# Chunked delta-rule scan: product order, PSUM banks, activation tables and a moved residual add

## The reference

```python
def step(S, xs):
    qk_i, qd_i, kd_i, u_i, w_i, gl_i = xs
    v_new = u_i - jnp.einsum('bhid,bhde->bhie', w_i, S)
    o_i = jnp.einsum('bhid,bhde->bhie', qd_i, S) + jnp.einsum('bhij,bhje->bhie', qk_i, v_new)
    S = S * gl_i[..., None, None] + jnp.einsum('bhid,bhie->bhde', kd_i, v_new)
    return S, o_i

S0 = jnp.zeros((B, H, dk, dv), q.dtype)
...
o_dn = o_dn * lax.rsqrt(jnp.mean(jnp.square(o_dn), axis=-1, keepdims=True) + RMS_EPS)
...
return jnp.concatenate([o_attn, o_dn], axis=-1) @ w_out
...
h = layer_norm(DEEPNORM_ALPHA * h + mix, ln1_g, ln1_b)
ffn = peer_ffn(h, peer_w_query, peer_sub_keys, peer_u, peer_v)
h = layer_norm(DEEPNORM_ALPHA * h + ffn, ln2_g, ln2_b)
```

## Time and profile before

| | |
|---|---|
| median of 3 runs | 3115.99 us (3113.97 to 3116.4) |
| the profiled execution | 3117.14 us |
| its span, first to last instruction | 3115.3 us |
| PE, DVE, ACT, POOL busy | 2386.0, 2232.4, 1148.3, 1183.5 us |
| gathers (queue q0) | 1073.81 MB, 83.5% of the DMA engines' span |
| other loads (q1) | 154.32 MB, 12.6% |
| mean granted TensorE clock | 0.877 of full speed |

### The profile page before, as it was taken

One profiled execution on the slowest core, in us unless ns is written; L12 is line 12 of the kernel. 1 busy time (PEld: TensorE's weight loads), 2 busy tenths in 40 slices (PEclk: granted clock), 3 DMA queues, 4 the chain that ended last, 5 costly groups with the idle time before them and its releaser, 6 DMA issues.

```text
span 3115.3 us, 37879 instructions
## 1 busy us (share of the span) xinstructions
PE 2386.0 (77%) x11858; PEld 1345.3 (43%) x11858; DVE 2232.4 (72%) x5639; ACT 1148.3 (37%) x3506; POOL 1183.5 (38%) x1028
## 2 busy tenths in 40 slices
PE   8897778868789687877879778886878668785554
PEld 7684435434356343543446443542435324351111
DVE  5388656986579766797568966689656986678644
ACT  4123533354323533235333353324533354333222
POOL 0033442344423444234533445234542344434442
PEclk9999989889899797888888889888989879888777
DMA  8189999999999999999999999999999999999997
GB/s 348 41 345 418 420 419 403 402 417 420 420 404 406 420 415 416 408 386 420 420 407 414 413 420 422 401 389 407 420 420 404 402 416 420 416 386 419 411 422 311
DMA packets 189000, 1235.90 MB, mean 397 GB/s; under 512 B 21752, under 2 KB 21880, under 8 KB 54656
## 3 DMA queue, kind: packets, MB, share of 16 engines
q0 software_dynamic: 147456, 1073.81, 83.5%
q1 hardware_dynamic: 39168, 154.32, 12.6%
q10 hardware_dynamic: 2176, 5.36, 0.4%
HBM read 1229.21 MB, written 4.19 MB: 396 GB/s over the span
## 4 chain that ended last, share of the span: by engine, by line
PE 31%; DVE 31%; DMA 20%; ACT 7%; issue 7%; POOL 2%; another core or an unknown queue 1%; DVEq 0%; ACTq 0%; POOLq 0%; SPq 0%
DMA ring<-in_uv,expert_used 18%; DVE ring L1823 14%; PE expert_sum L989 13%; PE bank L612 7%; PE bank L601 2%; POOL ring L539 2%; ACT diag L1314 2%; PE bank L619 2%; DVE arena L1454 1%; DMA chunk<-in_weights 1%; PE bank L593 1%; DVE conv L1474 1%; PE bank L742 1%; DVE arena L1469 1%
## 5 line engine op out<-in xcount | busy, mean ns | idle before, releaser
L539 POOL DMA_INDIRECT ring<-in_uv,expert_used x1024 | 1183.3, 1156 | 1895.4 <-PE expert_sum L989 1387.0
L989 PE MATMUL expert_sum<-ring,diag 128*64 128x512 f32 x4096 | 1185.3, 708 | 623.9 <-ACT diag L1314 618.9
L1823 DVE CUSTOM_DVE_ANT_0 ring<-ring,x_pair 128x1024 f32<-128x1024 f32 x1024 | 1221.4, 1223 | 357.2 <-DMA ring<-in_uv,expert_used 351.5
L989 PEld LDWEIGHTS expert_sum<-ring,diag 128*64 128x64 f32 x4096 | 308.7, 154 | 1246.2 <-issue 1230.3
L1307 ACT ACTIVATE h_raw<-h_raw 128x2 f32<-128x2 f32 x512 | 104.2, 204 | 1341.8 <-DVE h_raw L1823 1320.0
L1314 ACT ACTIVATE diag<-const,h_raw 128x64 f32<-128x64 f32 x1024 | 292.8, 333 | 6.2 <-PE expert_sum L989 5.8
L1310 ACT ACTIVATE h_raw<-h_raw,gate_used 128x1 f32<-128x1 f32 x1024 | 245.6, 286 | 16.7
L612 PEld LDWEIGHTS bank<-oT,chunk 128*128 128x128 f32 x1344 | 152.7, 192 | 22.7 <-issue 22.7
L612 PE MATMUL bank<-oT,chunk 128*128 128x128 f32 x1344 | 158.6, 277 | 0.0
L1454 DVE MAX8 arena<-arena 128x8 f32<-128x128 f32 (+1 forms) x384 | 103.8, 326 | 48.4 <-ACT arena L1260 43.1
L601 PE MATMUL bank<-chunk,oT 128*128 128x256 f32 x464 | 109.7, 387 | 0.0
(11 more groups left out here) (275 smaller groups left out, 2715.1 us busy)
## 6 DMA issues: line engine op xcount, KB each, us to landing
chunk<-in_weights SPq DMA_DIRECT2D x228, 512.0 KB
ring<-in_weights SPq DMA_DIRECT2D x17, 1024.0 KB, 23.8
ring<-in_uv,expert_used POOLq DMA_INDIRECT x1024
chunk<-in_weights SPq DMA_DIRECT2D x4, 1024.0 KB, 20.7
x<-in_x SPq DMA_DIRECT2D x8, 512.0 KB
out<-oT ACTq DMA_DIRECT2D x8, 512.0 KB
o_cat<-in_xT SPq DMA_DIRECT2D x7, 512.0 KB
xT_even<-in_xT SPq DMA_DIRECT2D x4, 512.0 KB
```

Source lines behind the costliest of these rows:

```text
L539: pool.indirect_dma_start(out=place(n, j), out_offset=None, in_=io["uv"], in_offset=bass.IndirectOffsetOnAxis(ap=expert_used[:, j:j + 1], ...
L989: mm = pe.matmul(expert_sum[i][c * SPAN:(c + 1) * SPAN, :], diag[:, (j % DIAGS) * SPAN:(j % DIAGS + 1) * SPAN], place(n, j)[:, D + i * 512 ...
L1823: dve.tensor_tensor_reduce(u, u, x_pair[:, (j % 2) * D:(j % 2 + 1) * D], 1.0, 0.0, ALU.mult, ALU.add, h_raw[:, j:j + 1]).then_inc(dotted.s ...
```

## The change

PE issues Q.S right behind W.S, before it waits for the subtraction, and each head's output gets a bank of its own (`O_BANKS`), so that Q.S of all heads comes first and QK.V of all heads later. In chunk 0 K.V comes before QK.V, in chunk 1 behind it. DVE's state update waits for Q.S (`q_state`) in place of QK.V. ACT copies four pieces, one from each bank. In block 0, chunk 0, the state is zero: W.S, Q.S and the subtraction are left out, and A_U is used as v_new. `add_half` of block 0 moves behind `dn_out` in DVE's queue. Ahead of the wait for each of the three roots ACT gets an instruction that loads a table set named `natural_log_exp_and_others`.

```diff
+        O_BANKS = (2, 0, 1, 5)
@@ PE, scan
-                bw, bo, bk = 3, 2, 4
+                bw, bk = 3, 4
                 for c in range(2):
                     rows = slice(c * CHUNK, (c + 1) * CHUNK)
                     if c == 0:
@@
                         pe.wait_ge(*state_new.at(n, 1))
                         pe.wait_ge(*o_copied.at(n, 1))
-                    each_head(bank[bw], tile(A_WT), state[:, :]).then_inc(w_state.sem, 1)
+                    from_zero = early and c == 0
+                    if from_zero:
+                        pe.sem_inc(w_state.sem, 1)
+                        pe.sem_inc(q_state.sem, 1)
+                    else:
+                        each_head(bank[bw], tile(A_WT), state[:, :]).then_inc(w_state.sem, 1)
+                        for h in range(DH):
+                            hs = slice(h * P, (h + 1) * P)
+                            mm = pe.matmul(bank[O_BANKS[h]][:, 0:P], tile(A_QDT)[:, hs], state[:, hs], start=True, stop=False)
+                        mm.then_inc(q_state.sem, 1)
                     mark(("ws0", "ws1")[c])
                     spare(early, (2, 1)[c])
                     pe.wait_ge(*v_new.at(n, c + 1))
+                    vn = tile(A_U) if from_zero else tile(A_VN)
+
+                    def into_state():
+                        for h in range(DH):
+                            hs = slice(h * P, (h + 1) * P)
+                            mm = pe.matmul(bank[bk][:, hs], tile(A_KDEC)[rows, hs], vn[rows, hs], start=True, stop=True)
+                        mm.then_inc(kv_done.sem, 1)
+
+                    if c == 0:
+                        into_state()
                     for h in range(DH):
                         hs = slice(h * P, (h + 1) * P)
-                        mm = pe.matmul(bank[bk][:, hs], tile(A_KDEC)[rows, hs], tile(A_VN)[rows, hs], start=True, stop=True)
-                    mm.then_inc(kv_done.sem, 1)
-                    for h in range(DH):
-                        hs = slice(h * P, (h + 1) * P)
-                        pe.matmul(bank[bo][:, hs], tile(A_QDT)[:, hs], state[:, hs], start=True, stop=False)
-                        mm = pe.matmul(bank[bo][:, hs], tile(A_QKT)[rows, hs], tile(A_VN)[rows, hs], start=False, stop=True)
+                        mm = pe.matmul(bank[O_BANKS[h]][:, 0:P], tile(A_QKT)[rows, hs], vn[rows, hs], start=from_zero, stop=True)
                     mm.then_inc(o_done.sem, 1)
+                    if c == 1:
+                        into_state()
@@ ACT, scan and roots
-                    act.copy(tile(A_O)[rows, :], bank[2][rows, :]).then_inc(o_copied.sem, 1)
+                    for h in range(DH):
+                        ins = act.copy(tile(A_O)[rows, h * P:(h + 1) * P], bank[O_BANKS[h]][rows, 0:P])
+                    ins.then_inc(o_copied.sem, 1)
@@
+                act.preload_act_table_set("natural_log_exp_and_others")
                 act.wait_ge(*o_ms.at(n, 1))
@@
+                act.preload_act_table_set("natural_log_exp_and_others")
                 act.wait_ge(*var_ready.at(n, 1))
@@ DVE, scan
-                    dve.wait_ge(*solved_copied.at(n, 1))
-                    dve.wait_ge(*w_state.at(n, c + 1))
-                    tt(tile(A_VN)[rows, :], tile(A_U)[rows, :], bank[bw][rows, :], ALU.subtract).then_inc(v_new.sem, 1)
+                    if n == 0 and c == 0:
+                        dve.sem_inc(v_new.sem, 1)
+                    else:
+                        dve.wait_ge(*solved_copied.at(n, 1))
+                        dve.wait_ge(*w_state.at(n, c + 1))
+                        tt(tile(A_VN)[rows, :], tile(A_U)[rows, :], bank[bw][rows, :], ALU.subtract).then_inc(v_new.sem, 1)
                     mark(("ws0", "ws1")[c])
                     dve.wait_ge(*kv_done.at(n, c + 1))
-                    dve.wait_ge(*o_done.at(n, c + 1))
+                    dve.wait_ge(*q_state.at(n, c + 1))
@@
-                if n == 0:
-                    add_half(0, expert_sum)
                 dve.wait_ge(*o_copied.at(n, 2))
@@
                 tt(by_head(o_cat[:, 512:1024]), by_head(tile(A_O)), over_cols(col(S_RT, DH), P), ALU.mult).then_inc(dn_out.sem, 1)
+                if n == 0:
+                    add_half(0, expert_sum)
```

More of the change, by code:

```diff
@@ L343, in build @@
         w_state = signal("w_state", 2)
+        q_state = signal("q_state", 2)
         v_new = signal("v_new", 2)
```

## The result

The changed kernel takes **3095.19 us** (median of 4 runs, 3092.87 to 3100.25) against 3116.19 for the kernel before beside it (3113.97 to 3119.75): a ratio of 0.9939, 95% interval 0.9926 to 0.9953, so 21.0 us faster. The forecast was 3106.6 with a range down to 3101: right in direction, and short by half. The profiled execution took 3092.87 us, 24.3 less than that of before.

The account below looks back on a forecast made before the run. Bytes pace 2915 us between a latency chain before 166 us and a latency tail. Gains 7.6 (block 0) + 1.3 (tail) + 0.5 (middle) = 9.4 us, from the median 3115.99 to 3106.6 us; range 3101 to 3112.

Parts of the forecast that it names:

- Block 0: Start of the kernel, up to the first gather: 6.8 us at the transposes and 0.8 at the first norm, 7.6 together.
- the output transposes: Block 0, behind the scan: 6.8 us earlier, taken between 5.9 and 7.1.
- the norm: Block 0's first norm: its table load goes, but keep-busy matmuls stand before x1's transposes, so -0.8 us, not -1.28.
- Tail: End of the kernel: the table load between Ln and Exp of the last norm goes, -1.3 us.
- Scan stages: Scans of blocks 1 to 7: DMA share stays at 1.0, time saved there is spent waiting for the next gather.
- The middle: The 2915 us paced by bytes, between first and last gather: -0.5 us.
- I take -0.5: The value in us chosen for the part paced by bytes, as the saved loads and scan lie beside transfers.
- an earlier norm does not bring that gather earlier: Turns between blocks: DVE last waits 1.9 to 2.6 us for the old block's gather before making the new indices.
- The upper bound: Part paced by bytes, at best: seven turns following the norm, 9.0 us, and a stretch such as 1572 to 1587, 2.6.
- the middle gains too: Rival, chance 0.10: the turns follow the earlier norm, sum 18.4 us or half of the 9.0, 3098 to 3102 us.
- The rule on the most contended engine: Whole kernel: a change that leaves DMA alone gives nothing, 3116 us; said to agree for the middle, not before 166 us.
- the limit of telling: Whole kernel: a measurement can tell 0.2%, 6.2 us, so faster means below 3109.8 us.

Follow-up runs that it names:

- root_after_turn: The kernel before with the table set of both functions loaded ahead of the second norm's root only: 3111.37 us, ratio 0.9993.
- after_norm_late: The changed kernel with the load ahead of the first norm replaced in blocks 1 to 7 by two loads behind the variance wait: 3098.80 us, ratio 0.9955.
- after_sums_late: The changed kernel with VectorE reading the expert sums twice at the turns into blocks 1 to 7: 3112.65 us, ratio 0.9999.
- after_again: The changed kernel itself measured once more, nothing changed: 3096.78 us, ratio 0.9949.

## Why the prediction was right at the ends and wrong in the middle

- **Block 0, right.** 7.6 us were forecast, 8.0 measured from the scan to the first gather. The copies end at 103.57 instead of 110.11, 6.5 earlier (6.0); the output transposes come 7.6 earlier (6.8), because the copies were done earlier and the norm rows ran only partly at the low clock (5.83 us, not 6.9); the norm gave 0.6 behind that (0.8), held by the keep-busy group as foreseen. Chunk 1's W.S starts 4.0 us after TensorE's two spare products at 95.23 (4.3 forecast, 7.8 before). The four copies took 0.75, not 0.9. add_half is hidden. Of the loads 24 are gone. An agreement to 0.4 us is in part luck: two executions of the same block 0 took 70.8 and 72.9 us (before and root_after_turn).
- **Tail, right.** 1.3. The Trainium skill puts a drain of 1.38 us on top of the load at each switch ("ScalarE: Activation LUTs", "What ACT_TABLE_LOAD costs"), by which the tail would have given 2.7. The runs do not agree: in after_norm_late the second of two loads starts 1.29 us behind the first, and Ln 1.29 behind that.
- **Scan stages, right as far as it went.** Their DMA share stayed at 1.01, as said.
- **The middle, wrong.** The step that failed is "I take -0.5", by way of "an earlier norm does not bring that gather earlier". That sentence is true: the last gather of the old block still comes last before the new indices, with a wait of 2.5 to 3.6 us in the changed kernel. But it is not the only wait of the turn. The read of the sums comes behind the indices, ends on TensorE and not on a gather, and stood late by 0.7 to 6.8 us in each turn; the earlier trace rows show the turn's other wait. In its place the runs showed that the middle gains from an earlier norm: the two loads ahead of the turn gave it some 4 us, all three loads 6, the scan alone 7, all together 8 to 12 by the medians. In the profiled pair it was 13.5. That it goes by way of the late read is shown where VectorE was held 2.8 us longer at each turn; for the smaller lateness of 0.4 to 2 us it is not shown. The upper bound was even in the text, 9.0 for the turns and 2.6 behind the scan, 11.6 in all; the value was taken from the wrong end of it.
- **The rival "the middle gains too"** was the right one, for its reason too, the turns following the earlier norm, and had a chance of 0.10. Its price, 9.0 us or half of it, was too small at the upper measurement: the wait that went was 25 us over the eight reads, and in the profiled pair the middle fell by 13.5, block 3's stall included.
- **The rule on the most contended engine** (the Trainium skill, "Perfetto Trace Analysis", "Identifying the Most-Contended Engine"), read as the prediction reads it, that a change which leaves DMA alone gives nothing, does not agree with the middle, against what the prediction said of it: after_sums_late left DMA alone as well, and it cost 16 to 19 us.

What stays open is how much of the middle's gain is the stalls at the low clock; they were not tried by themselves. Before's trace has one and the changed kernel's none, but after_again has one as well, with a middle of 2591.4, so they do not look like the whole of it. Open is also why three of before's eight reads, those at the turns into blocks 2, 5 and 6, came so late (the 25.8 us of "remote"): they wait for a signal that only TensorE gives, yet the records of its last pair end 2.2 to 2.9 us before them.

## What to carry to other kernels

A stage with its transfer queues full is not safe to be costed at nothing: between full stages lie hand-overs, and each wait of a hand-over has to be read with its releaser, those that come behind the next stage's first transfer as well as the last one ahead of it. An engine that is 95% busy for the next 80 us has little room to make good a late start: here 2.8 us more of its work at each hand-over cost 0.7 to 3.8 us in each of blocks 1 to 6, while 0.4 to 1.8 us of lateness in after_norm_late's blocks 2, 4 and 6 cost nothing, and being earlier than the changed kernel gave at most 3 us in all. Where two unlike savings each give about the same and together hardly more, look for the one wait that both relieve, and before a wait is given the price, look block by block whether the time was lost where the wait grew.

## What the runs showed of the hardware that was not expected

The granted clock of TensorE fell inside the busy part of before: in block 3's top-k stage TensorE had waited 2.43 us for ScalarE's diagonals, then the clock fell to the low level (1.2 GHz) during the next pair of experts, and the group of 16 eight-column products behind it took 3.58 us instead of 1.95. The wait does not settle it: the changed kernel's TensorE waited 2.42 us at the same place and stayed at the full level. In blocks 1, 3 and 5 of the fourteen traces it waited 2.4 to 2.6 us within 4 us ahead of these products every time, and in 12 of the 42 the group took 3.58 or 3.59 us; what decides it, no run here shows. First before, then the changed kernel:

```profile
1332.90 2.74 PE L989 MATMUL expert_sum<-ring,diag 128*64 128x512 f32 x8 [2.43 <-ACT diag L1314]
1335.57 3.58 PE L649 MATMUL bank<-w_ba,xT_even 128*128 128x8 f32 x16
```
```profile
1321.44 1.94 PE L1007 MATMUL expert_sum<-ring,diag 128*64 128x512 f32 x8 [2.42 <-ACT diag L1336]
1323.31 1.95 PE L651 MATMUL bank<-w_ba,xT_even 128*128 128x8 f32 x16
```

The stretch of before lost 40% of its transfers while GpSimd waited for a ring slot, and the same stretch of the changed kernel stayed at the full level (granted clock and DMA share are the last numbers but one):

```profile
1330.00:1340.00 10.00, 7.57 (x29) 4.90 (x28) 9.64 (x42) 2.85 (x11) 2.41 (x2) 0.70 1.02 417
1340.00:1350.00 10.00, 10.00 (x44) 7.27 (x43) 9.49 (x28) 2.60 (x10) 1.79 (x2) 0.79 0.59 224
```
```profile
1347.91 0.94 POOL L539 DMA_INDIRECT ring<-in_uv,expert_used  x1 [8.81 <-PE expert_sum L989]
```
```profile
1320.00:1330.00 10.00, 8.56 (x46) 5.80 (x48) 9.64 (x42) 3.99 (x15) 2.03 (x2) 1.00 1.01 406
1330.00:1340.00 10.00, 10.00 (x54) 7.08 (x51) 9.49 (x28) 2.90 (x13) 2.95 (x3) 1.00 0.98 383
```

Matmuls that alternate between starting a sum and adding to it took 0.21 us per record; the same products as two streams take 0.12 to 0.13. Four 64x128 copies on ScalarE took 0.75 us together, against 0.58 for one of 64x512. And executions of one kernel spread by 13 us here (before from 3106.49 to 3119.51 in 25 runs, and by 17 in another 26), twice what the text took for the limit of telling, so that single profiles differ by as much as the parts of this change.
